# One decoder layer with attention, a gated recurrence and PEER: first stage two chunks deep, and all low parts up to norm 1 on VectorE

## What is computed

```python
ada = jax.nn.silu(c) @ w_ada[l] + b_ada[l]
sh1, sc1, gt1, sh2, sc2, gt2 = jnp.split(ada[:, None, :], 6, axis=-1)
h = x * (1.0 + sc1) + sh1
proj = h @ w_in[l]
qa, ka, va, hq, hf, hi, hg, ga, gb = jnp.split(proj, split_at, axis=-1)
ya = moba_attention(qa, ka, va)             # 8 heads of 64, causal, ALiBi
yb = hgrn2(hq, hf, hi, hg, lb, norm_g)      # gated recurrence, 4 heads of 128
mixed = sigmoid(ga) * (ya @ w_branch_a[l]) + sigmoid(gb) * (yb @ w_branch_b[l])
x = layer_norm(DEEPNORM_ALPHA * x + gt1 * (mixed @ w_out[l]), ln1_g[l], ln1_b[l])   # norm 1
h2 = x * (1.0 + sc2) + sh2
y = peer(h2, peer_wq[l], peer_subkeys[l], peer_u[l], peer_v[l])
x = layer_norm(DEEPNORM_ALPHA * x + gt2 * y, ln2_g[l], ln2_b[l])
```

## Time and profile before

| | |
|---|---|
| median of 3 runs | 1073.29 us |
| lowest, highest | 1073.18, 1073.39 us |
| the profiled execution's own time | 1073.39 us |
| its span, first to last instruction | 1071.7 us |
| mean granted clock of TensorE | 0.989 |
| TensorE busy | 1041.0 us (97%) |
| VectorE busy | 724.2 us (68%) |
| ScalarE busy | 518.2 us (48%) |
| GpSimd busy | 375.0 us (35%) |

### The profile page before, as it was taken

How to read it: one execution, slowest core, us unless ns; L and a number is a source line. 1 busy time by engine, 2 the same in 40 slices (tenths; PEclk the granted TensorE clock), 3 DMA queues, 4 the chain that set the end, 5 groups by cost and what they waited for, 6 DMA issues and landing times.

```text
span 1071.7 us, 18291 instructions
## 1 busy us (share of the span) xinstructions
PE 1041.0 (97%) x7154; PEld 965.5 (90%) x7154; DVE 724.2 (68%) x1594; ACT 518.2 (48%) x786; POOL 375.0 (35%) x179
## 2 busy tenths in 40 slices
PE   7899999998999999999999999999999999999996
PEld 7899888997999999999999999998888888888875
DVE  5869998766699039646667677765555755666556
ACT  4685745535444454544443433345554445554442
POOL 1035323100687878876666666600001000000002
PEclk9999999988999999999999999999999999999999
DMA  9857846644455555544444444455668567776651
GB/s 358 320 189 255 287 159 228 222 157 155 150 172 181 174 180 183 187 158 142 140 149 135 145 139 139 139 175 190 195 190 330 175 212 241 244 237 207 194 175 43
DMA packets 57050, 204.92 MB, mean 191 GB/s; under 512 B 6658, under 2 KB 8706, under 8 KB 56194
## 3 DMA queue, kind: packets, MB, share of 16 engines
q1 hardware_dynamic: 55252, 198.50, 56.5%
q0 software_dynamic: 1424, 5.24, 1.3%
q10 hardware_dynamic: 288, 0.01, 0.0%
HBM read 201.63 MB, written 2.10 MB: 190 GB/s over the span
## 4 chain that ended last, share of the span: by engine, by line
PE 87%; DVE 7%; ACT 3%; issue 2%; DMA 1%; SPq 0%; ACTq 0%; DVEq 0%
PE px L1073 32%; PE pw L780 15%; PE pw L781 14%; PE pw L782 14%; PE px L1045 5%; DVE acc L1136 1%; DVE w_lo L1124 1%; PE px L1011 1%; DMA raw<-in_w 1%; ACT w_hi L494 1%; PE px L844 1%; ACT a_hi L531 0%; PE pv L780 0%; PE pv L781 0%; PE pv L782 0%
## 5 line engine op out<-in xcount | busy, mean ns | idle before, releaser
L494 ACT ACTIVATE w_hi<-raw 128x1024 fp32r<-128x1024 f32 x312 | 328.3, 1056 | 333.9 <-PE px L1073 171.4
L421 POOL TENSOR_TENSOR w_lo<-raw,w_hi 128x1024 fp32r<-128x1024 f32 x146 | 356.6, 2443 | 275.8 <-ACT w_hi L494 156.5
L780 PE MATMUL pw<-a_hi,w_hi 128*128 128x256 f32 x1280 | 370.1, 289 | 2.1 <-DVE a_lo L1362 2.1
L782 PE MATMUL pw<-a_hi,w_lo 128*128 128x256 f32 x1280 | 362.7, 283 | 0.0
L781 PE MATMUL pw<-a_lo,w_hi 128*128 128x256 f32 x1280 | 362.6, 283 | 0.0
L1124 DVE TENSOR_TENSOR w_lo<-raw,w_hi 128x1024 fp32r<-128x1024 f32 x166 | 203.0, 1225 | 158.5 <-ACT w_hi L494 155.3
L780 PEld LDWEIGHTS pw<-a_hi,w_hi 128*128 128x128 f32 x1280 | 246.0, 192 | 3.8 <-DVE a_lo L1362 2.5
L781 PEld LDWEIGHTS pw<-a_lo,w_hi 128*128 128x128 f32 x1280 | 246.2, 192 | 0.1
L782 PEld LDWEIGHTS pw<-a_hi,w_lo 128*128 128x128 f32 x1280 | 245.8, 192 | 0.0
L1073 PE MATMUL px<-w_hi,ws_hi 128*128 128x512 f32 x512 | 159.4, 390 | 0.9 <-DVE ws_lo L1514 0.9
L1073 PE MATMUL px<-w_hi,ws_lo 128*128 128x512 f32 x512 | 159.0, 389 | 0.0
(11 more groups left out here) (326 smaller groups left out, 1146.4 us busy)
## 6 DMA issues: line engine op xcount, KB each, us to landing
raw<-in_u SPq DMA_DIRECT2D x128, 512.0 KB, 3.7
raw<-in_v SPq DMA_DIRECT2D x128, 512.0 KB, 4.7
raw<-in_ws SPq DMA_DIRECT2D x56, 512.0 KB, 4.7
ada<-in_w_ada SPq DMA_DIRECT2D x32, 512.0 KB, 6.6
raw<-in_w SPq DMA_DIRECT2D x8, 768.0 KB, 9.8
ada<-in_ada SPq DMA_DIRECT2D x6, 1024.0 KB, 10.6
ada<-in_ada SPq DMA_DIRECT2D x4, 512.0 KB, 4.8
x_nat<-in_x SPq DMA_DIRECT2D x1, 1024.0 KB, 8.6
```

The costliest lines, as they stand in the source:

```text
L421: nc.gpsimd.tensor_tensor(w_lo[:, m % RING], raw[:, m % RING], w_hi[:, m % RING].bitcast(F32), ALU.subtract) \
L494: return nc.scalar.activation(out, in_, ACT.Copy, **kw)
L780: nc.tensor.matmul(out, lh, rh, start=start and x == 0, stop=False)
L782: last = nc.tensor.matmul(out, ll, rh, start=False, stop=stop and x == len(pairs) - 1)
```

## The change

It has two parts.

In the first stage, the sum of a chunk is made in two halves: steps 0 to 3 (`early`) of chunk c + 2 behind `lo1` of chunk c + 1, and steps 4 to 7 (`late`) of chunk c + 1 right behind `h_lo(c)`. TensorE makes `mod1(c + 1)` after three blocks, no longer after four. `xT` is loaded by eight transfers, one to a chunk, where three were. Chunk 0's weights are loaded and split in two halves of 768 columns. The chain of `lb` moves ahead of the first sum, with a semaphore of its own for its load. ScalarE's clearings of `acc` and the two bias loads are gone: the first step of each `acc` sum (k = 0) is a plain scaling, and the biases are added at the end, those of `gt1` from a broadcast load (512 KB into `gt1` itself, issued at block 24) and those of `mod2` from two more groups of columns in `ln_cols`.

In blocks 6 to 23 VectorE makes the second piece's low part too, right behind the first one's. GpSimd keeps the masking of `aT`.

```diff
@@ -45,7 +45,6 @@
-POOL_LO = range(FIRST, 24)
@@ -133,7 +132,7 @@
-        ln_cols = small("ln_cols", 2 * KC)
+        ln_cols = small("ln_cols", 4 * KC)
@@ -346,9 +346,8 @@
-            def load_x(i):
-                q = (slice(0, 1), slice(1, 4), slice(4, 8))[i]
-                sp.dma_start(xT[:, q], xT_d.rearrange("(k p) t -> p k t", p=P)[:, q]).then_inc(x_chunk_landed[i], 16)
+            def load_x(c):
+                sp.dma_start(xT[:, c], xT_d[c * P:(c + 1) * P]).then_inc(x_chunk_landed[c], 16)
@@ -358,20 +357,17 @@
-            def load_bias(g):
-                sp.wait_ge(acc_cleared, g + 1)
-                sp.dma_start(acc[0:1, g], b_ada_d[0:1, (g + 1) * 2 * ADA_W:(g + 2) * 2 * ADA_W]).then_inc(bias_landed[g], 16)
...
-            for c in range(KC):
+            load_ada1(0)
+            sp.dma_start(raw1[0][:, 0:FW // 2], w1_d[0][:, 0:FW // 2]).then_inc(raw1_landed[0], 16)
+            load_x(0)
+            sp.dma_start(raw1[0][:, FW // 2:FW], w1_d[0][:, FW // 2:FW]).then_inc(raw1_head_landed, 16)
+            for c in range(1, KC):
                 load_ada1(c)
-                if c < 3:
-                    load_x(c)
+                load_x(c)
...
-            for g in range(2):
-                load_bias(g)
@@ -383,6 +379,9 @@
+                    sp.wait_ge(o_done, TT)
+                    sp.dma_start(gt1[:, :], b_ada_d[0:1, 2 * D:3 * D].rearrange("a n -> (a n)").partition_broadcast(P)) \
+                        .then_inc(gt1_bias_landed, 16)
@@ -441,17 +440,11 @@
-            for b in POOL_LO:
-
-                pool.wait_ge(lo_ready, used(b, 0))
-                split_lo(2 * (b - FIRST) + 1)
-                if b == 14:
-
-                    pool.wait_ge(aT_copied, TT)
-                    nc.gpsimd.affine_select(out=aT[:, :, :, :].rearrange("p a h t -> p (a h) t"),
-                                            in_=aT[:, :, :, :].rearrange("p a h t -> p (a h) t"),
-                                            compare_op=ALU.is_ge, fill=0.0, base=0,
-                                            pattern=[[0, TT * HG], [1, P]], channel_multiplier=-1).then_inc(aT_ready, 1)
+            pool.wait_ge(aT_copied, TT)
+            nc.gpsimd.affine_select(out=aT[:, :, :, :].rearrange("p a h t -> p (a h) t"),
+                                    in_=aT[:, :, :, :].rearrange("p a h t -> p (a h) t"),
+                                    compare_op=ALU.is_ge, fill=0.0, base=0,
+                                    pattern=[[0, TT * HG], [1, P]], channel_multiplier=-1).then_inc(aT_ready, 1)
@@ -504,7 +497,7 @@
-            act.dma_start(lb_raw[:, :], lb_d).then_inc(small_landed, 16)
+            act.dma_start(lb_raw[:, :], lb_d).then_inc(lb_landed, 16)
@@ -514,6 +507,13 @@
+                if c == 0:
+                    q = slice(0, FW // 2)
+                    copy(hi1[0][:, q], raw1[0][:, q]).then_inc(hi1_ready, 1)
+                    act.wait_ge(raw1_head_landed, 16)
+                    q = slice(FW // 2, FW)
+                    copy(hi1[0][:, q], raw1[0][:, q]).then_inc(hi1_ready, 1)
+                    return
@@ -521,7 +521,7 @@
-                act.wait_ge(x_chunk_landed[0 if c == 0 else 1 if c < 4 else 2], 16)
+                act.wait_ge(x_chunk_landed[c], 16)
@@ -533,12 +533,6 @@
-                if c in (2, 4):
-                    act.wait_ge(consts, 1)
-                    nc.scalar.activation(acc[:, c // 2 - 1].rearrange("p (a b) -> p a b", b=P),
-                                         ones_pp[:, :].unsqueeze(1).broadcast_to([P, 2 * ADA_W // P, P]), ACT.Copy, scale=0.0) \
-                        .then_inc(acc_cleared, 1)
@@ -865,7 +859,7 @@
-                    if b == 3 and c + 1 < KC:
+                    if b == 2 and c + 1 < KC:
@@ -1126,30 +1120,40 @@
-                if t in (0, 2 * KC):
-                    dve.wait_ge(bias_landed[third], 16)
...
-                v.scalar_tensor_tensor(a, ada[:, t % ADA_SLOTS], sc_col[:, k:k + 1], a, ALU.mult, ALU.add).then_inc(ada_done, 1)
+                if k == 0:
+                    ins = v.tensor_scalar(a, ada[:, t % ADA_SLOTS], sc_col[:, k:k + 1], None, ALU.mult)
+                else:
+                    ins = v.scalar_tensor_tensor(a, ada[:, t % ADA_SLOTS], sc_col[:, k:k + 1], a, ALU.mult, ALU.add)
+                ins.then_inc(ada_done, 1)
             def split_lo1(c):
-                dve.wait_ge(hi1_ready, c + 1)
+                if c == 0:
+                    for h in range(2):
+                        q = slice(h * FW // 2, (h + 1) * FW // 2)
+                        dve.wait_ge(hi1_ready, h + 1)
+                        ins = v.tensor_tensor(lo1[0][:, q], raw1[0][:, q], hi1[0][:, q].bitcast(F32), ALU.subtract)
+                    ins.then_inc(lo1_ready, 1)
+                    return
+                dve.wait_ge(hi1_ready, c + 2)
...
-            def sum_part(c):
+            def sum_part(c, ks):
                 s = c % CHUNK_SLOTS
-                dve.wait_ge(ada1_landed[s], 16 * (c // CHUNK_SLOTS + 1))
-                if c >= 2:
-                    dve.wait_ge(mod1_done, c - 1)
-                for k in range(KC):
+                if ks[0] == 0:
+                    dve.wait_ge(ada1_landed[s], 16 * (c // CHUNK_SLOTS + 1))
+                    if c >= 2:
+                        dve.wait_ge(mod1_done, c - 1)
+                for k in ks:
@@ -1160,7 +1164,8 @@
-                ins.then_inc(part_ready, 1)
+                    if k == KC - 1:
+                        ins.then_inc(part_ready, 1)
@@ -1169,22 +1174,31 @@
-            dve.wait_ge(small_landed, 32)
+            dve.wait_ge(lb_landed, 16)
...
+            dve.wait_ge(lb_e_ready, 1)
+            link(v.tensor_tensor(lb_max[:, :], lb_e[:, 0:HG], lb_e[:, HG:2 * HG], ALU.add))
+            link(v.reciprocal(lb_max[:, :], lb_max[:, :]))
+            link(v.tensor_tensor(lb_col[:, :], lb_e[:, 0:HG], lb_max[:, :], ALU.mult))
+            v.tensor_scalar(om_lb[:, :], lb_col[:, :], -1.0, 1.0, ALU.mult, ALU.add)
+            early, late = range(4), range(4, KC)
+            sum_part(0, early)
+            dve.wait_ge(small_landed, 16)
...
+            sum_part(0, late)
+            split_lo1(0)
             for c in range(KC):
-                sum_part(c)
-                split_lo1(c)
+                h_lo(c)
                 if c == 0:
-                    dve.wait_ge(lb_e_ready, 1)
-                    link(v.tensor_tensor(lb_max[:, :], lb_e[:, 0:HG], lb_e[:, HG:2 * HG], ALU.add))
-                    link(v.reciprocal(lb_max[:, :], lb_max[:, :]))
-                    link(v.tensor_tensor(lb_col[:, :], lb_e[:, 0:HG], lb_max[:, :], ALU.mult))
-                    link(v.tensor_scalar(om_lb[:, :], lb_col[:, :], -1.0, 1.0, ALU.mult, ALU.add))
-                h_lo(c)
+                    sum_part(1, early)
+                if c + 1 < KC:
+                    sum_part(c + 1, late)
+                    split_lo1(c + 1)
+                if c + 2 < KC:
+                    sum_part(c + 2, early)
@@ -1202,10 +1216,8 @@
-                    if b - 1 in POOL_LO:
-                        dve.wait_ge(lo_ready, used(b - 1))
                     split_lo(2 * (b - FIRST))
-                    if b not in POOL_LO and not BRANCH <= b - 2 < BRANCH + 4:
+                    if not BRANCH <= b - 2 < BRANCH + 4:
@@ -1313,8 +1325,9 @@
-                    v.tensor_copy(gt1[:, 0:512], px[0][:, :])
-                    mark(v.tensor_copy(gt1[:, 512:1024], px[1][:, :]), gt1_ready, 1)
+                    dve.wait_ge(gt1_bias_landed, 16)
+                    v.tensor_tensor(gt1[:, 0:512], px[0][:, :], gt1[:, 0:512], ALU.add)
+                    mark(v.tensor_tensor(gt1[:, 512:1024], px[1][:, :], gt1[:, 512:1024], ALU.add), gt1_ready, 1)
@@ -1331,8 +1344,9 @@
-                        v.tensor_copy(mod2[:, 0:KC], px[2][:, 0:KC])
-                        link(v.tensor_scalar(mod2[:, KC:2 * KC], px[2][:, KC:2 * KC], 1.0, None, ALU.add))
+                        v.tensor_tensor(mod2[:, 0:KC], px[2][:, 0:KC], ln_cols[:, 2 * KC:3 * KC], ALU.add)
+                        link(v.scalar_tensor_tensor(mod2[:, KC:2 * KC], px[2][:, KC:2 * KC], 1.0, ln_cols[:, 3 * KC:4 * KC],
+                                                    ALU.add, ALU.add))
@@ -1629,7 +1643,8 @@
-        "ln1_cols": np.concatenate([a[k][0].reshape(KC, P).T for k in ("ln1_b", "ln1_g")], axis=1),
+        "ln1_cols": np.concatenate([y.reshape(KC, P).T for y in (a["ln1_b"][0], a["ln1_g"][0], a["b_ada"][0, 3 * D:4 * D],
+                                                                 a["b_ada"][0, 4 * D:5 * D])], axis=1),
...

```

More of the change, by code:

```diff
@@ L257, in layer @@
         ada1_head_landed = sem("ada1_head_landed")
-        bias_landed = [sem(f"bias_landed{g}") for g in range(2)]
-        x_chunk_landed = [sem(f"x_chunk_landed{i}") for i in range(3)]
+        x_chunk_landed = [sem(f"x_chunk_landed{c}") for c in range(KC)]
+        raw1_head_landed = sem("raw1_head_landed")
         ada1_landed = [sem(f"ada1_landed{s}") for s in range(CHUNK_SLOTS)]
@@ L270, in layer @@
```

(3 more changed lines are left out.)

## The result

The kernel after took 1064.64 us (median of four runs, 1064.31 to 1065.06), the kernel before on the same chip 1073.34. The ratio is 0.9913, with an interval of 0.9896 to 0.9930: 8.7 us faster, 0.1 us from the forecast. The profiled execution took 1064.31 us, its span is 1062.6. Runs of one kernel differ: the 35 runs of the kernel before that were made beside the experiments took from 1071.9 to 1076.4 us. A profile is one such run. The sum is right; not all of its terms are, and the traces tell which.

What follows compares the result with a forecast made beforehand. TensorE, busy for 1041.0 of 1071.7 us, was taken as the bound, with VectorE next. 1073.4 less 6.2 (first stage) and 2.6 (low parts) gave 1064.6, 1064.5 us after 0.1 to the median; range 1063 to 1066.5.

Steps and rivals of the forecast that it cites:

- The sum: Whole kernel: 1073.4 less 6.2 us for the first stage and 2.6 for low parts, 1064.5 us after 0.1 to the median.
- The period: First stage, steady chunks: `mod1` after three blocks and the halved sum cut 6.13 us to 5.43, 0.71 less, six times.
- The start: First stage: VectorE is the bound, chunk 1 starts at 19.3 us instead of 21.24, a gain of 1.94 us.
- the first matmul: Chunk 0: earlier `lb` chain and later wait for `b_cols` bring it to 12.35 us instead of 13.76.
- 1.2 us more if half of the 18 matmuls run at the low clock ... not later than VectorE: Chunk 0: TensorE ready for chunk 1 at 19.0 us even with that 1.2 us, against VectorE's 19.1.
- The low parts: Blocks 6 to 23: VectorE's load stays within 1 us or falls; TensorE waits less for `prob`, 2.6 us, bounds 0 and 4.2.
- Transfers: First stage loads: 4.7 us a chunk fits the period; nothing taken, worst 1.5 us, or 2 us if a fixed cost shows.
- The clock behind `mod2`: From 216.1 to 252.3 us: the clock's fall only moves, no change taken, 1.7 us allowed either way.
- rival 1: The clock falls for a shorter time behind `mod2`, 1.7 us less: 1062.8 us; chance 0.14.
- Rival 4: Blocks 6 to 23: VectorE becomes the bound between 62 and 173 us, overflowing by 8.9 us, slower: 1076.0 us; chance 0.03.
- Rival 2: Only one part pays: first stage held by loads or VectorE, or `prob` waits return otherwise; about 1067 us; chance 0.17.
- rival 3: First stage: TensorE's idle time stays, `part` or `lo` being late; only the start's 1.9 us won, 1071.4 us; chance 0.04.

Runs made afterwards that it cites:

- e5: Kernel after with `mod1` of the next chunk again after four blocks instead of three; 1068.43 us, ratio 0.9944.
- e6: Kernel after with each chunk's sum made in one piece behind `a_lo`, `mod1` still after three blocks; 1066.51 us, ratio 0.9928.
- e9: Kernel after, unchanged, run and profiled once more; 1063.32 us, ratio 0.9902.
- e3: Kernel after plus one unused two-input GpSimd instruction for each of 18 blocks, and a clearing of `echo`; 1075.11 us, ratio 1.0001.
- e1: Kernel before with only the 18 second low parts of blocks 6 to 23 moved to VectorE; 1070.38 us, ratio 0.9964.
- e2: Kernel after with the 18 low parts back on GpSimd, so the first stage's part alone; 1069.05 us, ratio 0.9954.
- e4: Kernel after plus 6 matmuls of ones ahead of chunk 0's `mod1` and 7 behind it; 1063.72 us, ratio 0.9906.
- e8: e4 plus matmuls of ones in norm 1: 8 ahead of its transposes, 3 between row tiles, 7 behind; 1061.71 us, ratio 0.9887.
- e10: e8 once more, run beside e9; 1061.70 us, ratio 0.9883.
- e11: e4 with `xT` loaded by three transfers instead of eight; 1064.46 us, ratio 0.9911.

## Why the prediction was right, and where it wasn't

**The period.** 5.42 us for a forecast 5.43. e5 gives the 0.71 us back when `mod1` moves one block later, e6 gives 0.68 back when the sum is in one piece. Both halves of the argument hold, and the six periods are worth 6 x 0.71 = 4.3 us.

**The start.** The forecast let chunk 1 gain 1.94 us. e9 has 1.70, with 12.63 for the first matmul and 19.54 for chunk 1. There VectorE and TensorE's path are even: VectorE's sum ends at 18.87 us, `xT` is ready at 18.94, and `a_lo` starts at 18.97. The first profile has -0.52. The step that failed is "1.2 us more if half of the 18 matmuls run at the low clock ... not later than VectorE". In both profiles all 18 did, which in e9 cost 1.5 us (3.72 us from the first of them to `mod1`, where a later chunk has 2.23). In the first profile `mod1` (1.70 us instead of 0.95) and 15 of the 18 behind it did too, and TensorE, not VectorE, set the start of chunk 1: 21.76 us where 19.3 was forecast. I had taken the length of the fall from one execution as if it belonged to the kernel. The 0.24 us at the first matmul are another miss: `om_lb` took 0.92 us at 5.46 and ended with GpSimd's clearing of `aT` (5.40 to 6.35); in the kernel before it took 0.17. Not every VectorE instruction beside that clearing is held up: `lb_max`, also on 128x4 elements, took 0.16 us at 5.93. That the clearings hold up the scalings is borne out by e3, where one more of them made the next two scalings longer by another 0.7 us. No run takes apart what the earlier `lb` chain and the halved load of chunk 0 gave each.

**The low parts.** Measured 3.07 us, in e1, after and e9 alike, for a forecast 2.6. The waits for `prob` went from 2.8 to 0.2 us as written. The other 0.5 us: side by side, the three matmuls that waited for `prob` come 2.8 us sooner, not 2.6, and three matmuls with weights at 94.2, 94.5 and 101.3 us come 0.1 us sooner each, too little for a row of the waits. I had summed only what has a row. That the move is free for VectorE was right: its busy time fell.

**Transfers.** "Nothing" was right for the change as a whole, for a reason of which I had given only a part. `hi` of chunk 1 started at 14.16 (forecast 14.05), and the eight small loads are worth 1.0 to 1.8 us: in three they would have taken that out of the first stage.

**The clock behind `mod2`.** Forecast: no change, 1.7 us either way. It gave 1.65 us behind `mod2` (low from 215.9 to 219.3 after, from 221.6 to 228.4 before), just rival 1, and 0.45 us in norm 1. e9 repeats the first (1.63) and not the second (-0.01). Of the twelve profiles of other kernels than before, nine have the short fall behind `mod2`, e2 has none, e3 and e5 have the long one; and the kernel before has one profile, so its long fall is a single draw. I don't credit the change with it. That it came from the change is neither shown nor excluded.

**The sum.** -2.3 for the start, +0.5 for the low parts, +2.1 for the clock: three errors that all but cancel. The low stretches of the clock add up to 26.1 us in the profile before and in the one after, at other places: longer in chunk 0, shorter behind `mod2` and in norm 1. e9 has 22.7 us of them. With the fall of e9 the same kernel gave 10.7 us in its profile (1062.64). That the forecast of 1064.5 came within 0.1 us is luck. The range was less so: the other median of this kernel, 1063.32, lies in it as well. But its allowance of 1.7 us was for the clock behind `mod2`, and the fall in chunk 0, which was worth 2.1 us, had none.

**The rivals.** Rival 4 had the right mechanism for a kernel that keeps the collisions: e3 has the same VectorE work and no gain, at 1075.1 us. That this is near its 1076.0 proves little, since e3's profile also has a later start and the longest falls of the clock. In the change the collisions went with the instructions. Rival 1's fall did come, but its 1062.8 us didn't, since the start gave 2.3 us less. Rival 2 is excluded by the waits for `prob` and the period, rival 3 by the period.

## What to carry over

Work out each engine's own time for one turn of a loop; the loop can't go below the largest, and a long serial sum needs only its last half inside it. Before an instruction is left on GpSimd to spare VectorE, count the VectorE instructions that it holds up: here 18 instructions on GpSimd cost more than doing their work on VectorE. And before a profile's difference is credited to an edit, compare the granted clock in both and profile the same kernel twice: one fall of the clock was worth 2.1 us, a quarter of the effect.

## What the runs showed of the hardware

- One kernel, two executions: the granted clock was at its lower level for 10.2 us in chunk 0 in one and for 3.4 us in the other. With thirteen matmuls of ones around the eight small ones it stayed up, in e4, e8, e10 and e11 alike.
- 18 instructions of GpSimd of 2.7 us each cost TensorE 8.7 us in the stretch in which VectorE was the next bound (e3; up to 1.7 us of it by a fall of the clock), and made a `prob` scaling of 0.29 us one of 1.13 us on average.
- A scaling of 128x4 elements on VectorE took 0.92 us beside GpSimd's clearing of a tile, and 0.17 us without it; a two-input instruction of that size took 0.16 us beside the same clearing. With a second clearing behind the first, in e3, the next two scalings, of 128x256, took 1.97 us instead of 1.23.
- From the start of eight one-column matmuls to `a_lo`, two steps of ScalarE later, it took 2.73 us where TensorE had been waiting and 2.62 us where it came out of other matmuls.
